# Gate product ahead of the inverse root in the recurrence heads, and the last head's output tiles in two parts

## The reference

```python
def mixer_hgrn2(u, mem_kv, w_in, lb_fwd, lb_bwd, norm_g, w_out):
    q, i, zf, zb, gate, xq = jnp.split(u @ w_in, ...)
    ...
    o = (gla_chunked(q, k_f, v, lf_f)
         + flip_t(gla_chunked(flip_t(q), flip_t(k_b), flip_t(v), flip_t(lf_b))))
    o = rmsnorm(o, norm_g.reshape(HG_HEADS, HG_VAL_DIM))     # per head, 128 values
    o = o * jax.nn.silu(gate)
    return jnp.concatenate([o, memory_cross_attn(xq, mem_kv)], axis=-1) @ w_out
```

## Time and profile before

| what | us |
|---|---|
| median of 3 runs | 2363.16 |
| lowest and highest | 2363.08, 2364.33 |
| the profiled execution | 2364.11 |
| its span in the profile | 2362.3 |
| TensorE busy | 2343.5 |
| GpSimd busy | 1626.6 |
| VectorE busy | 1172.0 |
| ScalarE busy | 648.9 |

### The profile page before, as it was taken

One profiled execution on the slowest core, in us unless ns is written; L12 is line 12 of the kernel. 1 busy time (PEld: TensorE's weight loads), 2 busy tenths in 40 slices (PEclk: granted clock), 3 DMA queues, 4 the chain that ended last, 5 costly groups with the idle time before them and its releaser, 6 DMA issues.

```text
span 2362.3 us, 31444 instructions
## 1 busy us (share of the span) xinstructions
PE 2343.5 (99%) x11270; PEld 1913.5 (81%) x11270; DVE 1172.0 (50%) x1967; ACT 648.9 (27%) x1250; POOL 1626.6 (69%) x2225
## 2 busy tenths in 40 slices
PE   9999999999999999999999999999999999999998
PEld 7877778888888888767788888887888887888887
DVE  4336654333301224577358553045888885765501
ACT  3233321002201212455221110025667653111111
POOL 8664558777877877657569887763454447988873
PEclk9999999999999999999999999999999999999999
DMA  4233223333333333222223333322222222323332
GB/s 172 89 102 96 81 81 98 96 94 97 98 98 96 93 123 98 81 72 90 72 81 98 98 98 98 96 84 64 71 72 72 72 63 81 97 94 96 98 98 72
DMA packets 63407, 214.41 MB, mean 91 GB/s; under 512 B 6688, under 2 KB 10912, under 8 KB 63136
## 3 DMA queue, kind: packets, MB, share of 16 engines
q1 hardware_dynamic: 60528, 206.55, 28.4%
q10 hardware_dynamic: 2736, 5.96, 0.8%
HBM read 210.38 MB, written 2.10 MB: 90 GB/s over the span
## 4 chain that ended last, share of the span: by engine, by line
PE 49%; DVE 3%; ACT 1%; issue 0%; POOL 0%; DVEq 0%
PE acc L599 12%; PE acc L601 12%; PE acc L600 12%; PE acc L974 1%; PE acc L973 1%; PE acc L972 1%; PE ps_o L786 1%; PE ps_s L1176 1%; PE ps_s L744 1%; PE ps_s L599 1%; PE ps_s L600 1%; PE ps_s L601 1%; PE ps_s L1165 0%; PE ps_o L1235 0%; PE ps_s L973 0%; PE ps_s L974 0%
## 5 line engine op out<-in xcount | busy, mean ns | idle before, releaser
L564 POOL TENSOR_TENSOR w_lo<-w_raw,w_hi 128x256 fp32r<-128x256 f32 (+1 forms) x1532 | 1207.0, 819 | 188.8 <-ACT w_hi L1657 175.1
L558 POOL CAST w_hi<-w_raw 128x512 fp32r<-128x512 f32 x688 | 435.7, 662 | 511.6 <-DMA w_raw<-stream 472.4
L599 PE MATMUL acc<-h_hi,w_hi 128*128 128x512 f32 x1701 | 676.8, 398 | 0.9 <-DVE h_lo L1777 0.9
L601 PE MATMUL acc<-h_hi,w_lo 128*128 128x512 f32 x1701 | 663.4, 390 | 0.0
L600 PE MATMUL acc<-h_lo,w_hi 128*128 128x512 f32 x1701 | 662.5, 389 | 0.0
L599 PEld LDWEIGHTS acc<-h_hi,w_hi 128*128 128x128 f32 x1701 | 320.0, 188 | 68.7 <-issue 2.9
L601 PEld LDWEIGHTS acc<-h_hi,w_lo 128*128 128x128 f32 x1701 | 319.2, 188 | 67.7
L600 PEld LDWEIGHTS acc<-h_lo,w_hi 128*128 128x128 f32 x1701 | 319.8, 188 | 65.1 <-issue 2.2
L1349 ACT ACTIVATE probs<-probs,neg_max 128x256 f32<-128x256 f32 (+5 forms) x160 | 86.9, 547 | 129.0 <-DVE neg_max L1890 129.0
L1855 DVE TENSOR_TENSOR hid_tmp<-acc,rstd_in 128x512 f32<-128x512 f32 x82 | 56.7, 692 | 130.3 <-PE acc L601 128.1
L599 PE MATMUL acc<-u_hi,w_hi 128*128 128x512 f32 x256 | 99.6, 389 | 0.0
(11 more groups left out here) (436 smaller groups left out, 3943.6 us busy)
## 6 DMA issues: line engine op xcount, KB each, us to landing
w_raw<-stream SPq DMA_DIRECT2D x384, 512.0 KB, 3.5
toeplitz<-ext_in ACTq DMA_DIRECT2D x16, 256.0 KB, 2.8
out<-x_res SPq DMA_DIRECT2D x8, 256.0 KB, 2.4
x_res<-x_in SPq DMA_DIRECT2D x3, 512.0 KB, 7.5
mem<-mem_in ACTq DMA_DIRECT2D x1, 1024.0 KB, 6.8
consts<-consts_in SPq DMA_DIRECT2D x1, 656.0 KB, 9.4
x_res<-x_in SPq DMA_DIRECT2D x2, 256.0 KB, 5.2
rope<-rope_in ACTq DMA_DIRECT2D x1, 512.0 KB, 7.7
```

The lines of the kernel that those rows point to most:

```text
L558: nc.gpsimd.tensor_copy(hi[:, half], raw[:, half]).then_inc(hi_made, 1)
L564: nc.gpsimd.tensor_tensor(lo[:, part], raw[:, part], f32(hi[:, part]), ALU.subtract).then_inc(low_quarter if not end else split_made if i ...
L599: nc.tensor.matmul(ps, hi, x_hi[:, k, 0:cols], start=(k == 0), stop=False)
L601: mm = nc.tensor.matmul(ps, lo, x_hi[:, k, 0:cols], start=False, stop=(k == st.kt - 1))
```

## The change

In all heads the gain and the gate are multiplied onto the PSUM output first (`head_gated`), into `o2`. Exp then writes the inverse root over `ps_o` and not into `ffn_tmp`; before it does, it waits for that product (`hg_gated`). `head_out` is one product of `o2` and `ps_o`. Ln no longer waits for the head before. `head_gated(h - 1)` stands behind the first score copy of turn `h`; in the last turn it stands behind the backward queries, ahead of the backward levels. The high halves of heads 0 to 5 on ScalarE wait for `o_taken` at the count that TensorE had for that head.

For the last head, the high half is written as a product of its own (`hg_last_hi`), then the unrounded product goes into `ps_o`, and the low half is their difference. TensorE's step 11 is cut in two: eight matmuls with the high half of the activations, which wait for the high half alone, and four with the low half.

```diff
@@ TensorE
+            def out_last_lead(k, done):
+                tile = k * BANKS
+                s, t = (st.first_slot + tile // SLOT_TILES) % RING, tile % SLOT_TILES
+                pe.wait_ge(hg_last_hi, 1)
+                for c in range(BANKS):
+                    ps = banks[st.banks[c]][:]
+                    nc.tensor.matmul(ps, w_hi[:, s, t + c, :], o_hi3[:, k, 0:T], start=False, stop=False)
+                    nc.tensor.matmul(ps, w_lo[:, s, t + c, :], o_hi3[:, k, 0:T], start=False, stop=False)
+                pe.wait_ge(o_ready, DT + 12 + k + 1)
+                for c in range(BANKS):
+                    mm = nc.tensor.matmul(banks[st.banks[c]][:], w_hi[:, s, t + c, :], o_lo2[:, k, 0:T], start=False, stop=True)
+                mm.then_inc(slot_done, done)
...
-            out_lead(11, done=1 + early // SLOT_TILES)
+            out_last_lead(11, 1 + early // SLOT_TILES)
@@ ScalarE
             def head_root():
                 act.wait_ge(sq_used, n["sq"])
-                if n["rstd"]:
-                    act.wait_ge(hg_normed, n["rstd"])
                 nc.scalar.activation(ffn_tmp[:, 1, :], ps_t[:], ACT.Ln, scale=1.0 / P, bias=small["eps_v"][:]).then_inc(hg_log, 1)
                 n["rstd"] += 1
                 act.wait_ge(hg_log, n["rstd"])
-                nc.scalar.activation(ffn_tmp[:, 1, :], ffn_tmp[:, 1, :], ACT.Exp, scale=-0.5).then_inc(hg_rstd, 1)
+                act.wait_ge(hg_gated, n["rstd"])
+                nc.scalar.activation(ps_o[:], ffn_tmp[:, 1, :], ACT.Exp, scale=-0.5).then_inc(hg_rstd, 1)
...
-                    act.wait_ge(hg_normed, i + 1)
+                    act.wait_ge(o_taken, taken_heads[i])
@@ VectorE
+            def head_gated(h):
+                dve.wait_ge(hg_silu_g, h + 1)
+                dve.wait_ge(sq_ready, squared_heads[h])
+                step.wait()
+                step(nc.vector.scalar_tensor_tensor(o2[:, X_HEADS + h, :], ps_o[:], param("b_norm_g", h), hg_in[h % 2][:, 4, :], ALU.mult, ALU.mult),
+                     hg_gated)
             def head_out(h):
                 dve.wait_ge(hg_rstd, h + 1)
                 step.wait()
-                step(nc.vector.scalar_tensor_tensor(o2[:, X_HEADS + h, :], ps_o[:], param("b_norm_g", h), ffn_tmp[:, 1, :], ALU.mult, ALU.mult),
-                     o_taken)
-                dve.wait_ge(hg_silu_g, h + 1)
-                step.wait()
-                step(nc.vector.tensor_tensor(o2[:, X_HEADS + h, :], o2[:, X_HEADS + h, :], hg_in[h % 2][:, 4, :], ALU.mult), hg_normed)
+                step(nc.vector.tensor_tensor(o2[:, X_HEADS + h, :], o2[:, X_HEADS + h, :], ps_o[:], ALU.mult), o_taken)
+            def last_head_out():
+                h, k = HG_HEADS - 1, X_HEADS + HG_HEADS - 1
+                o, hi = o2[:, k, :], o_hi3[:, k, 0:T]
+                head_gated(h)
+                dve.wait_ge(hg_rstd, h + 1)
+                step.wait()
+                step(nc.vector.tensor_tensor(hi, o, ps_o[:], ALU.mult), hg_last_hi)
+                step.wait()
+                step(nc.vector.tensor_tensor(ps_o[:], o, ps_o[:], ALU.mult), o_taken)
+                step.wait()
+                step(nc.vector.tensor_tensor(o_lo2[:, k, :], ps_o[:], f32(hi), ALU.subtract), o_ready)
...
                 head_queries(h, 1)
+                if h == HG_HEADS - 1:
+                    head_gated(h - 1)
                 head_levels(h, 1)
                 head_scores(h, 0)
+                if 0 < h < HG_HEADS - 1:
+                    head_gated(h - 1)
                 head_in(h + 1, 2)
...
             head_states(HG_HEADS - 1)
-            head_out(HG_HEADS - 1)
-            split_out(X_HEADS + HG_HEADS - 1, o_hi3)
+            last_head_out()
```

More of the change, by code:

```diff
@@ L434, in build @@
         hg_rstd = sem("hg_rstd")
-        hg_normed = sem("hg_normed")
+        hg_gated = sem("hg_gated")
+        hg_last_hi = sem("hg_last_hi")
         hg_o = sem("hg_o")
@@ L575, in _ @@
                 split(slot)
+        taken_heads = []
         @block.tensor
@@ L1237, in head_out @@
                 n["o"] += 1
+                taken_heads.append(n["o"])
             v0 = n["v"]
@@ L1278, in _ @@
             conv_mlp(1)
+        squared_heads = []
         @block.scalar
@@ L1608, in head_square @@
                 squared(ps_o[:], sq=ffn_tmp[:, 0:1, :])
+                squared_heads.append(n["sq"])
             def head_root():
                 act.wait_ge(sq_used, n["sq"])
-                if n["rstd"]:
-                    act.wait_ge(hg_normed, n["rstd"])
                 nc.scalar.activation(ffn_tmp[:, 1, :], ps_t[:], ACT.Ln, scale=1.0 / P, bias=small["eps_v"][:]).then_inc(hg_log, 1)
```

## The result

The changed kernel takes 2378.37 us (median of six runs, 2377.66 to 2379.6) against 2363.21 for the kernel before on the same chip (six runs, 2363.08 to 2372.9): ratio 1.0054 [1.0039, 1.007]. It is slower by 15.2 us, where I had forecast +1.3. The profiled executions agree: span 2376.8 against 2362.3, +14.5. A few executions of several of these kernels, as the 2372.9 here, are some 10 us longer than the rest for a reason that is not known, and the ratios, which are estimated over all runs, are not the quotients of the medians (that would be 1.0064 here).

What follows compares the result with a forecast made beforehand. The prediction took TensorE, busy 99% of the span, as the bound. Plus 2.4 us in turn 7 minus 1.1 at the last head gave +1.3: 2365.4 on the profiled execution, 2364.5 on the median, range 2362.2 to 2366.3.

Steps and rivals of the forecast that it cites:

- +1.3: Whole kernel: 2.4 us lost in turn 7 minus 1.1 us won at the last head.
- I cost it at nothing: Heads 0 to 5: Exp's 3.4 us delay on ScalarE is absorbed in its idle time, so no cost.
- 12.3 of idle time: ScalarE, each turn: busy 25.3 of 37.6 us, the idle 12.3 us absorbing the 3.4 us delay.
- the cover of a single pass: Turn 6: VectorE's levels end at 1888.30 and TensorE wants them at 1894.74, 6.4 us of cover.
- The table load runs under the wait: ScalarE ahead of Exp: the load runs during the wait, not after, so its 1.28 us adds nothing.
- the load waits too: Rival at head 6: load starts only after the gate product, Exp 1.3 us later; +2.6, 2365.8 us; chance 0.08.
- +2.4: Turn 7: VectorE's backward levels begin 2.4 us later, 0.8 product and 1.6 wait, reaching TensorE whole.
- -1.1: Last head: TensorE's wait with its restart at the last lead step goes entirely, winning 1.1 us.
- The zero for Exp into PSUM: ScalarE's Exp: writing PSUM takes no different time, from a 0.60 row against 0.63 into SBUF.
- Delay piles up over the heads: Rival in ScalarE's queue, turns 1 to 6: 3.4 us not absorbed each turn, +14 and +1.3, 2378; chance 0.02.
- no new waits of TensorE in turns 1 to 6: Expected trace sign: TensorE gets no new waits in the turns before turn 7.
- own range 2363.8 to 2365.5: Whole kernel: range of times in us given to the main forecast itself, with chance 0.68.

Runs made afterwards that it cites:

- swap_waits: The changed kernel with the two waits ahead of Exp written in the other order, hg_gated first and hg_log second; 2368.02 us, ratio 1.0015.
- heads_0_5: The kernel before with heads 0 to 5 alone in the new form, heads 6 and 7 old; 2374.65 us, ratio 1.0047.
- head_6_swap: The kernel before with head 6 alone in the new form and the two waits ahead of its Exp exchanged; 2366.04 us, ratio 1.0009.
- head_6: The kernel before with head 6 alone in the new form; 2367.99 us, ratio 1.0023.
- last_only: The kernel before with head 7 alone in the new form, its output tiles in two parts; 2361.88 us, ratio 0.9994.
- last_whole: Head 7 alone in the new form, but TensorE's step 11 in one piece as in the kernel before; 2362.02 us, ratio 0.9993.
- early_1_6: The changed kernel with the gate product of turns 1 to 6 moved behind the backward decays; 2367.96 us, ratio 1.0011.

## Why the prediction was wrong

**"I cost it at nothing", the six heads before: this step failed.** The delay of 3.4 us on ScalarE was sized rightly; setting it against "12.3 of idle time" was wrong. In the changed kernel that time lies in three pieces, each where ScalarE waits for somebody, and none between Exp and the exponential that VectorE's decays wait for. Nor was it one delay to be absorbed once. The edit added an edge from VectorE's end of turn to ScalarE, and the edge from ScalarE to VectorE's start of turn was there already; together they are a ring. I took the cover of a single pass (6.4 us to the levels) and didn't add up the cycle. From the changed kernel's rows it is 39.24, from swap_waits 37.91, against 37.63 of TensorE. Cost: 8.0 + 0.6 in the turns, and 2.7 of lateness at turn 7 (heads_0_5); together 11.3, where the medians of heads_0_5 give 11.1.

Most of the sum could have been made from the trace of the kernel before. ScalarE's work there from Exp to the end of the exponential that the decays wait for (L1679) is 16.5 (1849.26 to 1867.34, less the 1.6 of idle time in between), and VectorE's from the decays to the end of the score copy 19.8 (1869.38 to 1889.14); with the product and the gaps between instructions the ring comes to about 37.2, an estimate, and to 38.5 with a table load behind the product. Against 37.63 that leaves 0.5 us a turn with the load as I had it, not 12.3, and none with the load behind the product. The 37.91 measured in swap_waits shows that even the 0.5 wasn't there: the VectorE part took 0.9 longer, nearly all of it in two instructions that lie more under GpSimd's subtractions than before (the decays, 1.11 against 0.69, and the first level copy, 0.70 against 0.29).

**"The table load runs under the wait": this step failed too**, and the rival "the load waits too" holds. The row at 1946.95 showed a load ahead of an instruction with two waits, of which the one written last (for the head before) had long been met; it didn't show that a load never waits. With one wait alone, as Ln has in the changed kernel, the load runs ahead as well: it starts at 1962.60, and Ln at 1965.42. Price: 1.28 in every turn, so 10.3 in all with what hangs on it, and not the 1.3 that I gave the rival, as I saw it in turn 7 alone.
The Trainium skill, ScalarE: Activation LUTs, section "Step-by-step: what each stage is for", places the load right before its ACTIVATE and doesn't speak of waits. Read strictly, with the load behind the waits too, the trace agrees where the wait written last is the late one (1742.45, 1937.70) and doesn't where it is the other (1741.11 in swap_waits, 1946.95 in the earlier trace rows).
The Trainium skill, ScalarE: Activation LUTs, section "What ACT_TABLE_LOAD costs", adds about 1380 ns of drain to 1283 ns of load. The trace bears out the 1.28 alone: a load starts 0.08 behind the product's end, Exp 0.01 behind the load, and taking the load off the ring shortened the turn by 1.33.

**Turn 7, "+2.4": right for what it covered.** head_6_swap measured a lateness of +2.46, with waits in the two places named, and the levels under contention, taken as 5.27, came out at 5.34 there and 5.28 in the changed kernel. What stood on top in the changed kernel are the load (1.28; 1.43 between head_6 and head_6_swap), the lateness handed on (2.6 between head_6 and the changed kernel, 2.7 in heads_0_5), and the clock (1.35), which I hadn't thought of: a wait of 1.5 left it alone (1.00 in head_6_swap), that of 5.5 didn't.

**The last head, "-1.1": right**, -1.12 in the changed kernel. The zero for Exp into PSUM holds (0.60 against 0.63).

**"Delay piles up over the heads" ends at 2378, the time measured, but by luck and not by its mechanism.** It priced delays that add up until ScalarE's idle time is used; with 13.5 us of it unused, that does not happen. Its threshold (idle time under 3.4) was the wrong one, and with it the chance of 0.02. Also wrong was "no new waits of TensorE in turns 1 to 6": they stand at the keys, five of them that are new. The "own range 2363.8 to 2365.5" doesn't follow from the bounds given for turn 7 either: a lateness of 0.7 to 2.8 less 1.1 is 2362.8 to 2364.9. The measured time lies far outside of both.

No version beats the kernel before measurably. The best are last_only and last_whole, 1.7 and 1.6 below it, with intervals that reach past 1.

## What to carry to other kernels

When an edit makes engine A wait for B, look for the way back from A to B in the next turn of the loop, and add up the whole ring by rows; if it is longer than the bounding engine's turn, every turn pays, however idle A and B are. Idle time covers a delay only where it lies between the delayed instruction and the one somebody waits for. Where an instruction needs a table load and has two waits, write first the one that is met last, and look in the trace at which side of the load the idle time stands.

## What the runs showed of the hardware

The wait of 5.5 us cost TensorE more than its length. After idle times of 1.5, 1.8 and 2.7 us (head_6_swap, heads_0_5, swap_waits) the granted clock was 1.00 over the next four us; after 2.9, 3.9 and 5.5 us (head_6, early_1_6, the changed kernel) it was 0.65, 0.60 and 0.50, and the last of these cost 1.35 us that five matmuls of constants bought back. The row behind the wait of 2.7 us, to be set beside head_6's above:

```profile
1936.60:1940.60 4.00, 2.90 (x23) 2.66 (x24) 3.52 (x7) 0.60 (x1) 0.00 (x0) 1.00 0.01 2
```

Which side of a wait a table load falls on followed from the order in which two waits were written, with no other change to the program: 10.3 us here. With two waits the one written last held the load up, the one written first only the ACTIVATE; a wait that stood alone didn't hold the load up.
